# A streamed operand's last tile moved by 288 bytes in a two-block transformer kernel

## The reference, cut to what matters

```python
# first block
xn = rmsnorm(x, norm_mix_g)
q, k, v, xr, gr, ga, gb = split(xn @ w_in)              # 1024 -> 7168
ya = chunked_band_attention(q, k, v, rel_table) @ w_attn_out
yb = (rg_lru(conv(xr)) * gelu(gr)) @ w_rnn_out
h = x + (sigmoid(ga + b) * ya + sigmoid(gb + b) * yb) @ w_o
g, up = split(rmsnorm(h, norm_ffn_g) @ w_ffn_in)        # 1024 -> 2 x 2816
h = h + (silu(g) * up) @ w_ffn_out                      # 2816 -> 1024
h = rmsnorm(h, final_norm_g)
# second block
h = h + 0.5 * rms_norm(swiglu(rms_norm(h), ffn1_w_gu, ffn1_w_down))
z = rms_norm(h) @ w_in_2                                # 1024 -> 1952
h = h + rms_norm(concat(neighbourhood_attention(z), latent_attention(z)) @ w_out)
h = h + 0.5 * rms_norm(swiglu(rms_norm(h), ffn2_w_gu, ffn2_w_down))
```

## Time and profile before

| what | value |
|---|---|
| median of three runs | 935.5 us (935.29 to 937.14) |
| the profiled execution | 935.2 us |
| its span, first to last instruction | 933.4 us |
| TensorE busy (matmuls) | 925.4 us, 99% of the span |
| TensorE, weight loads | 840.3 us, 90% |
| VectorE | 593.8 us, 64% |
| ScalarE | 491.2 us, 53% |
| GpSimd | 301.2 us, 32% |
| DMA | 169.49 MB, mean 182 GB/s |

### The profile page before, as it was taken

The page is one execution under the profiler, slowest core; times in us unless marked ns, Lnnn a source line. Parts: engine busy times, 40 slices in busy tenths (PEclk is TensorE's granted clock), DMA queues, the critical chain, the costliest instruction groups (busy, mean ns, idle before and its releaser), DMA issues.

```text
span 933.4 us, 16744 instructions
## 1 busy us (share of the span) xinstructions
PE 925.4 (99%) x6268; PEld 840.3 (90%) x6268; DVE 593.8 (64%) x849; ACT 491.2 (53%) x765; POOL 301.2 (32%) x140
## 2 busy tenths in 40 slices
PE   9999999999999999999999999999999999999997
PEld 8999877788899999988999998888889889999886
DVE  6968977756656666723776666356486776666523
ACT  6688466644554444444644444447455654455441
POOL 0000000000145444544344445654441044445442
PEclk9999999999999999999999999999999999999999
DMA  8756675446556667785566665645513346666661
GB/s 257 247 180 185 202 234 160 134 161 199 162 158 190 191 184 230 238 253 184 180 197 187 184 199 190 229 151 168 181 47 113 111 148 190 190 201 196 185 201 67
DMA packets 132797, 169.49 MB, mean 182 GB/s; under 512 B 16731, under 2 KB 88446, under 8 KB 132614
## 3 DMA queue, kind: packets, MB, share of 16 engines
q1 hardware_dynamic: 132582, 168.67, 58.2%
q10 hardware_dynamic: 160, 0.07, 0.0%
HBM read 167.61 MB, written 1.10 MB: 181 GB/s over the span
## 4 chain that ended last, share of the span: by engine, by line
PE 98%; issue 1%; ACT 0%; DVE 0%; DVEq 0%; POOLq 0%; POOL 0%; ACTq 0%
PE acc L945 16%; PE acc L947 16%; PE acc L949 16%; PE acc L887 14%; PE acc L889 14%; PE acc L888 14%; PE tp L963 3%; PE acc L1298 1%; PE acc L1031 1%; PE sc L1253 1%; PE sc L1099 1%; PE tp L1118 1%; PE sc L981 1%; PE sc L1243 0%; ACT xt_hi L787 0%
## 5 line engine op out<-in xcount | busy, mean ns | idle before, releaser
L524 ACT ACTIVATE w_hi<-w_raw 128x1024 fp32r<-128x1024 f32 x300 | 316.6, 1058 | 284.4 <-PE acc L949 131.1
L2051 POOL TENSOR_TENSOR w_lo<-w_raw,w_hi 128x1024 fp32r<-128x1024 f32 x106 | 276.0, 2604 | 519.9 <-ACT w_hi L524 519.9
L1383 DVE TENSOR_TENSOR w_lo<-w_raw,w_hi 128x1024 fp32r<-128x1024 f32 x194 | 252.7, 1307 | 207.0 <-ACT w_hi L524 206.5
L945 PE MATMUL acc<-xt_hi,w_hi 128*128 128x256 f32 x1248 | 349.2, 280 | 0.0
L947 PE MATMUL acc<-xt_lo,w_hi 128*128 128x256 f32 x1248 | 348.3, 279 | 0.0
L949 PE MATMUL acc<-xt_hi,w_lo 128*128 128x256 f32 x1248 | 348.3, 279 | 0.0
L945 PEld LDWEIGHTS acc<-xt_hi,w_hi 128*128 128x128 f32 x1248 | 235.9, 189 | 1.2 <-issue 0.9
L949 PEld LDWEIGHTS acc<-xt_hi,w_lo 128*128 128x128 f32 x1248 | 235.7, 189 | 0.0
L947 PEld LDWEIGHTS acc<-xt_lo,w_hi 128*128 128x128 f32 x1248 | 234.5, 188 | 0.1
L887 PE MATMUL acc<-w_hi,hid_hi 128*128 128x512 f32 x264 | 103.0, 390 | 0.0
L889 PE MATMUL acc<-w_lo,hid_hi 128*128 128x512 f32 x264 | 102.8, 389 | 0.0
(11 more groups left out here) (228 smaller groups left out, 950.4 us busy)
## 6 DMA issues: line engine op xcount, KB each, us to landing
w_raw<-in_ffn_w_gu SPq DMA_DIRECT2D x172, 256.0 KB
w_raw<-in_w_in SPq DMA_DIRECT2D x68, 512.0 KB
w_raw<-in_w_ffn_in SPq DMA_DIRECT2D x88, 256.0 KB
w_raw<-in_ffn_w_down SPq DMA_DIRECT2D x44, 512.0 KB
w_raw<-in_w_ffn_out SPq DMA_DIRECT2D x22, 512.0 KB
w_raw<-in_w_rnn_out SPq DMA_DIRECT2D x8, 512.0 KB
w_raw<-in_w_attn_out SPq DMA_DIRECT2D x8, 512.0 KB
w_raw<-in_w_o SPq DMA_DIRECT2D x8, 512.0 KB
```

Source lines behind the costliest of these rows:

```text
L524: act.activation(w_hi[:, b, :], w_raw[:, b, :], ACT.Copy).then_inc(hi_done[b], 1)
L945: pe.matmul(o, w_hi[:, r, cols], xt1_hi[:, k, :], start=q == 0 and c == 2 * b and j == 0, stop=False, skip_group_check=True)
L1383: dve.tensor_tensor(w_lo[:, b, :], w_raw[:, b, :], w_hi[:, b, :].bitcast(F32), ALU.subtract).then_inc(lo_done[b], 1)
L2051: pool.tensor_tensor(w_lo[:, b, :], w_raw[:, b, :], w_hi[:, b, :].bitcast(F32), ALU.subtract).then_inc(lo_done[b], 1)
```

## The change

The view `xt1` of x keeps its place for tiles 0 to 6; tile 7 begins 72 elements (288 bytes) further on, in both the high and the low buffer. So it starts at 48 + 7 x 256 + 72 = element 1912 and ends at 2168 of 2176. All that reads or writes through `xt1_hi` and `xt1_lo` is affected, as the streamed operand and as the held one; the unshifted view `xt` is not. A small class gives the new places under the old indexing. No instruction, wait or transfer is added or removed.

```diff
+class Tiles:
+
+
+    def __init__(self, buffer, places):
+        self.buffer, self.places = buffer, places
+
+    def __getitem__(self, key):
+        rows, k, cols = key
+        at = self.places[k]
+        return self.buffer[:, at:at + T][rows, cols]
+
+
 def build(nc, a, out):
 
     top = [16896]
@@ -129,11 +141,11 @@
     w_hi = place("w_hi", [P, RING, SLAB], F32R)
     w_lo = place("w_lo", [P, RING, SLAB], F32R)
     h = place("h", [P, MT, D], F32)
-    shift = 48
+    places = [48 + k * T + (72 if k == KT - 1 else 0) for k in range(KT)]
     xt_hi_all = place("xt_hi", [P, KT * T + 128], F32R)
     xt_lo_all = place("xt_lo", [P, KT * T + 128], F32R)
-    xt_hi, xt1_hi = (xt_hi_all[:, at:at + KT * T].rearrange("p (k t) -> p k t", k=KT) for at in (0, shift))
-    xt_lo, xt1_lo = (xt_lo_all[:, at:at + KT * T].rearrange("p (k t) -> p k t", k=KT) for at in (0, shift))
+    xt_hi, xt_lo = (x[:, 0:KT * T].rearrange("p (k t) -> p k t", k=KT) for x in (xt_hi_all, xt_lo_all))
+    xt1_hi, xt1_lo = Tiles(xt_hi_all, places), Tiles(xt_lo_all, places)
```

## The result

The changed kernel takes 941.56 us (median of four runs, 941.26 to 941.98), the kernel before 935.39 us beside it (935.17 to 937.14). The ratio is 1.0062 with an interval of 1.0045 to 1.008: slower by 6.2 us. The forecast was 928.9, faster; it has the wrong sign. The value lies in the range (925.0 to 942.0), at 0.2 us from what the first rival gives with tile 7's own price at 0 (941.8). That it lies inside, by 0.4 us, owes to tile 7's small price: the first rival as the prediction priced it (944.6) lies outside.

What follows compares the result with a forecast made beforehand. TensorE's own matmul pace, in two stable rhythms, was taken as the bound. Profiled 935.2 us + 2.8 (tile 7's price) - 9.4 (slow stretches freed) = 928.6, set to 928.9 for the runs' median; range 925.0 to 942.0 us.

Steps and rivals of the forecast that it cites:

- What bounds the kernel: Whole kernel: TensorE's own matmul pace, no wait or clock; two stable rhythms 13.4 ns apart per triple.
- (a): Instructions: none added or removed, no wait or transfer; writes of tile 7 just go to other bytes, costed at nothing.
- (b): Matmuls holding x as weights, 54 of 432 on tile 7: 0 taken, with 0.1 or 0.9 us as other possibilities.
- (c): Tile 7 as moving operand, 480 matmuls in 40 streaming groups: up to 5.8 ns dearer each, +2.8 us taken.
- (d): Last slab of each streaming group: passages to and from tile 7 leave TensorE in the quick rhythm, net -9.4 us.
- jolts: Passages of the moving stream to and from tile 7, shifting it 288 bytes against the held operand, eight a group.
- the prediction's own sign of being wrong: First FFN: the forecast is wrong if a triple of matmuls there still takes 353 ns.
- Rival 1: Projections and third FFN, quick before: passages to tile 7 end in the slow rhythm, +6.3 and +2.8, 944.6 us; chance 0.22.
- Rival 2: Streaming stages keep their rhythms and only tile 7's own price of +2.8 us is paid: 938.3 us; chance 0.13.
- Rival 3: No effect: operands' places don't count for a single tile of eight, 935.5 us; chance 0.17.
- Rival 4: Half the effect: one FFN is freed and not the other, or only part of each group, about 932.8 us; chance 0.08.
- Cover: Streaming stages: the feed from ScalarE, VectorE and DMA keeps up with a faster TensorE, so nothing is late next.

Runs made afterwards that it cites:

- e4: Changed kernel with tile 7 moved by 64 bytes instead of 288, in both buffers and all streaming stages, to 0 modulo 256; 930.26 us.
- e10: Changed kernel with only the low buffer's tile 7 moved by 288 bytes, the high buffer as in the kernel before; 938.19 us.
- e7: Changed kernel with tile 7 moved by 128 bytes instead of 288, to 64 modulo 256; 932.37 us.
- e15: Changed kernel with tile 0 moved in place of tile 7, 192 bytes back to 0 modulo 256, in all streaming stages; 929.14 us.
- e17: Changed kernel with tile 0 in place of tile 7 at 0 modulo 256, in first and second FFN alone, other stages as before; 928.63 us.

## Why the prediction was wrong, point by point

- **What bounds the kernel.** Right. TensorE's pace was all there was, no wait came or went, and two rhythms in one and the same code are what the 6.2 us are made of.
- **(a) and (b).** Right. Instructions and waits are the same. Outside the four streaming stretches the span grew by 0.4 us in all (6.8 less 6.4), which holds group 0 and the held x, costed at 0 with 0.1 or 0.9 as other ends.
- **(c), tile 7's own price.** Too high for this change: the forecast took +2.8 us, 5.8 ns each, because 480 is nearer to 512 than to 192. Measured: the first FFN, slow before and after, grew by 0.2 us over 11 x 12 = 132 visited matmuls, 1.5 ns each; for all 480 that is 0.7, with the rounding of the starts 0.4 to 1.1. With every tile there the pace is 118.4 and not 119.1, and against the slow 117.8 this is next to nothing. A price must be set against the pace that surrounds it. Where the surroundings are quick, the size was right: with tile 7 at 0 modulo 256 (e4) the visits cost 1.9 to 2.6 ns a triple over 340.3, which over the 1280 triples of the 40 groups is an estimated 2.4 to 3.3 us.
- **(d), the rhythm.** This step failed. "If the jolts always leave it in the quick rhythm" was the choice that gave the sign, and nothing in the rows supported it over its opposite: the only disturbances there were interruptions, which had ended both ways. It was to give -9.4 us. Measured, the slow stretches got nothing back: the first FFN still takes 353.7 ns a triple, the prediction's own sign of being wrong. The quick ones turned slow, +1.8 us in the projections and +4.1 in the third FFN. The jolts do reset the rhythm, but a visit to 224 modulo 256 ends slow. The same kind of edit with 64, 192 or (tile 0) minus 192 bytes ends quick and comes near the forecast: 930.3, 930.9 and 929.1 us. Mechanism right, direction open and guessed.
- **Rival 1** came true where it said: after the visits to tile 7, in the projections (+1.8 us, forecast 1.7) and in the third FFN (+4.1, forecast 4.1). By the rows it deserved the forecast's chance, and had about half of it.
- **Rival 2** (rhythm untouched) is what the third and the first FFN show when the low part alone is moved (e10). That this run also took 938.2 us, near the rival's 938.3, is partly luck: its projections did turn slow. **Rival 3** is refuted by 1.0062 with an interval clear of 1. **Rival 4**, one FFN freed and not the other, is what visits to 64 gave in the profiled execution of e7. With x at 192, 224, 128 and 0 modulo 256 the same 256 columns took 113.3 or 117.8, 118.4, 118.7 and 120.0 ns. The Trainium skill (TensorE: Matmul & The Clock Gate, "Step-by-step: what each phase is for") says that loading the next weights takes nothing from the running matmul, and by that the four would be alike. The traces do not agree with it for this stream.
- **Cover.** "Nothing is late next" held: in the quick versions the streaming stages run at 340 to 344 ns a triple.

Open is why a visit at a distance of 0 or 128 throws the engine into the quick rhythm and one at 224 into the slow one. That two reads of the memory collide is what the dependence on distance suggests; no run shows the collision itself.

## What to carry to other kernels

Where one engine's pace is the bound and no wait is left, read the pace from starts, stage by stage: a pace that differs between stages with the same code is time to be had, here 10.0 of 935.5 us by the prediction's sum, of which e15 and e17 got 6 to 6.5. The distance of a matmul's two operands modulo 256 bytes is a knob that costs nothing and was worth up to 6.7 ns a matmul here (113.3 against 120.0); it must be tried on the chip, at several values and in several runs, since its sign can't be read from a trace that never visits the other place. A saving that hangs on a state left to chance at a stage's entry wants a reset in every group, as one tile at another place gave here.

## What the runs showed of the hardware that was not expected

- With operands 192 bytes apart modulo 256 the 256-column matmul has two stable rhythms, 113.3 and 117.8 ns; at 224, 128 and 0 the FFNs run at one pace each, 118.4, 118.7 and 120.0 ns. Distances 256 bytes apart are the same: 32 and 288 bytes gave 941.46 and 941.56 us.
- It is the distance and not the place: with weights and x both moved by 64 bytes both rhythms stayed, and the hidden tiles, which had not moved, went from 681 to 688 ns a triple.
- One program scattered from 933.1 to 942.2 us in ten runs at the same granted clock (0.999 to 1.0). The kernel before does it too, less: 930.88 to 937.14 us over all its runs. That it comes from the rhythm each stage enters is likely and not shown.
- At 192 bytes the page of the profile shows the rhythm without a single start being read: a matmul's duration of 276 or 281 ns, and weight loads of 188 with one line in three at 192 at the slow pace.
